# Chunk stage of a hybrid retention and RWKV-7 layer: low-rank products from rounded high parts with the rests stacked over the rows, and outputs and solves of two slabs issued alternately

## The reference, cut to what matters

```python
u = lp['rwkv_w0'][:, None, None, :] + jnp.einsum('btr,drc->dbtc', jnp.tanh(wd), lp['rwkv_w2'])
w = jnp.exp(-jnp.exp(-jax.nn.softplus(-u.astype(jnp.float32)) - 0.5))
a = jax.nn.sigmoid(lp['rwkv_a0'][:, None, None, :] + jnp.einsum('btr,drc->dbtc', ad, lp['rwkv_a2']))
...
def step(s, xt):
    wt, kt, vt, kkt, at = xt[:5]
    sa = jnp.einsum('bhvk,bhk->bhv', s, -kkt)
    s = (s * wt[:, :, None, :] + sa[..., None] * (kkt * at)[:, :, None, :]
         + vt[..., None] * kt[:, :, None, :])
    return s, jnp.einsum('bhvk,bhk->bhv', s, xt[5])
```

## Time and profile before

| what | value |
|---|---|
| median of 3 runs | 4121.16 us (4111.47 to 4129.18) |
| profiled execution, its own time | 4116.76 us |
| span of the profiled execution | 4114.9 us |
| granted TensorE clock, mean | 0.962 |
| busy: PE / DVE / ACT / POOL | 3772.4 / 2290.6 / 1947.2 / 613.5 us |
| chunk stage in the trace | about 1181 to 2225 us |

### The profile page before, as it was taken

The page is one execution under the profiler, slowest core; times in us unless marked ns, Lnnn a source line. Parts: engine busy times, 40 slices in busy tenths (PEclk is TensorE's granted clock), DMA queues, the critical chain, the costliest instruction groups (busy, mean ns, idle before and its releaser), DMA issues. The chain is left out here.

```text
span 4114.9 us, 93756 instructions
## 1 busy us (share of the span) xinstructions
PE 3772.4 (92%) x39634; PEld 3168.5 (77%) x39634; DVE 2290.6 (56%) x3788; ACT 1947.2 (47%) x3029; POOL 613.5 (15%) x601
## 2 busy tenths in 40 slices
PE   7999999999979899989898978997599999999993
PEld 6778878888868788888887767786488888888883
DVE  5533524434337777777776975455554545454445
ACT  5533434434336666666665443243144444444443
POOL 1000000000012122212210333200011111111111
PEclk9999999999989999999998989998699999999997
DMA  7566565555542222222323466654366666666667
GB/s 277 189 180 190 179 194 152 159 155 157 151 119 76 80 76 66 80 80 62 105 64 90 117 222 215 197 181 160 148 210 215 211 213 213 212 217 209 219 209 296
DMA packets 334966, 673.42 MB, mean 164 GB/s; under 512 B 32828, under 2 KB 213156, under 8 KB 316936
## 3 DMA queue, kind: packets, MB, share of 16 engines
q1 hardware_dynamic: 307592, 580.68, 43.3%
q0 software_dynamic: 27008, 87.46, 7.4%
HBM read 524.89 MB, written 143.15 MB: 162 GB/s over the span
## 5 line engine op out<-in xcount | busy, mean ns | idle before, releaser
L112 PE MATMUL fro__acc<-fro__hT_hi,fro__wh 128*128 128x512 f32 (+1 forms) x1608 | 626.0, 389 | 11.8 <-DVE fro__hT_lo L2671 8.9
L113 PE MATMUL fro__acc<-fro__hT_hi,fro__wl 128*128 128x512 f32 (+1 forms) x1608 | 614.3, 382 | 0.0
L114 PE MATMUL fro__acc<-fro__hT_lo,fro__wh 128*128 128x512 f32 (+1 forms) x1608 | 614.1, 382 | 0.0
L2677 DVE TENSOR_TENSOR fro__wl<-prj__w,fro__wh 128x1024 fp32r<-128x1024 f32 x201 | 246.2, 1225 | 640.6 <-ACT fro__wh L2460 640.6
L2088 DVE TENSOR_TENSOR fin__wl<-fin__raw,fin__wh 128x4096 fp32r<-128x4096 f32 x96 | 424.6, 4423 | 318.4 <-ACT fin__wh L2032 318.4
L2032 ACT ACTIVATE fin__wh<-fin__raw 128x4096 fp32r<-128x4096 f32 x96 | 348.4, 3629 | 190.4 <-PE exp__acc L114 190.3
L112 PE MATMUL exp__acc<-fin__wh,exp__xh 128*128 128x512 f32 x1024 | 400.9, 391 | 0.7 <-DVE exp__xl L2093 0.7
L113 PE MATMUL exp__acc<-fin__wh,exp__xl 128*128 128x512 f32 x1024 | 399.3, 390 | 0.0
L114 PE MATMUL exp__acc<-fin__wl,exp__xh 128*128 128x512 f32 x1024 | 399.2, 390 | 0.0
L112 PEld LDWEIGHTS fro__acc<-fro__hT_hi,fro__wh 128*128 128x128 f32 x1608 | 304.7, 189 | 77.9 <-issue 22.2
L113 PEld LDWEIGHTS fro__acc<-fro__hT_hi,fro__wl 128*128 128x128 f32 x1608 | 304.8, 190 | 59.2 <-issue 3.6
(11 more groups left out here) (460 smaller groups left out, 8121.9 us busy)
## 6 DMA issues: line engine op xcount, KB each, us to landing
fin__raw<-in_w_x SPq DMA_DIRECT2D x96, 2048.0 KB
prj__w<-in_w_z SPq DMA_DIRECT2D x201, 512.0 KB, 4.2
s_zT<-fro__pool SPq DMA_DIRECT2D x128, 256.0 KB, 4.7
fro__wm<-in_w_mod POOLq DMA_DIRECT2D x16, 1024.0 KB, 5.6
mix__gate<-s_zT SPq DMA_DIRECT2D x64, 256.0 KB, 4.3
prj__xin<-in_tokens SPq DMA_DIRECT2D x18, 512.0 KB, 5.4
rwc__kS<-s_kS SPq DMA_DIRECT2D x36, 256.0 KB, 3.1
rwc__kkn<-s_kkn SPq DMA_DIRECT2D x36, 256.0 KB, 3.3
```

Source lines behind the costliest of these rows:

```text
L112: pe.matmul(out, sh, mh, start=first, stop=False)
L113: pe.matmul(out, sl, mh, start=False, stop=False)
L114: return pe.matmul(out, sh, ml, start=False, stop=last)
L2677: ve.tensor_tensor(wl[s % 3][:, :, :], w[s % 3][:, :, :], wh[s % 3][:, :, :], ALU.subtract).then_inc(split_lo, 1)
```

## The change

- The operands of the low-rank products become fp32r. Rounded high parts and the rests are stacked over the 128 rows: `lowA` is the rounded weights twice over the rows (from `low_raw`), `zA` the rounded data above and its rest below; `lowB` holds the rest of the weights above, and the bias (rounded in row 64, its rest in row 96) below; `zB` holds the data above and the ones below. Each product of the four becomes two fp32r matmuls that add up in `PB[1]`.
- The parts of the weights are made once (`lowA` on ScalarE, `lowB` on VectorE, `low_parts`), before the first slab. They come by 8 DMAs a direction instead of 4.
- For every slab GpSimd casts `zS` into `zA` (`rounded_rows`), and VectorE makes `zB` and the rest in `zA` with two instructions of 128x256 (`rounded_rows`), after `centred`. The slab's data is loaded by `load_low`, two DMAs as before, one slab earlier.
- `D2`, `e_bk`, `e_rho`, `e_al`, `av`, `kd`, `bb` and `bon` move into `hold["tab"]`, and the loads for the next stage are issued at `h == LAST`.
- `outputs(h-2, 1)` no longer stands between `double(2, h)` and `couple(3, h)`. Where both exist, `outputs_and_solve` issues the eight products of `outputs(h-2, 1)` and the eight of `solve(h-1, 0)` by turns, at the place of `solve`.

```diff
@@ sync @@
+            def load_low(j):
+                for s in range(2):
+                    sp.dma_start(zS[j % 2][side(s), :, :], T["waS"][:, ds(slab_at(j), C)].rearrange("(k p) t -> p k t", k=2)).then_inc(lws[j % 2], 16)
...
             low_rank(1)
             low_rank_rows(1)
+            load_low(1)
             load(1)
+            sp.wait_ge(S["rlo"], at("rlo", 0))
+            load_low(2)
...
-                if h == SLABS - 6:
+                if h == LAST:
+                    for n in ("betad", "kappad", "al", "rho", "bonm"):
+                        sp.wait_ge(S[n], at(n, LAST))
@@ scalar @@
+            for d in range(2):
+                act.wait_ge(low_in[d], 128 + START)
+                act.activation(lowA[:, d, :, :], low_raw[d][:, :, :], ACT.Copy).then_inc(low_hi, 1)
             decays(0)
@@ vector @@
+            def low_parts(d):
+                ve.wait_ge(low_hi, d + 1 + START)
+                ve.tensor_tensor(lowB[0:64, d, :, :], low_raw[d][0:64, :, :], lowA[0:64, d, :, :], ALU.subtract).then_inc(low_lo, 1)
+                ve.wait_ge(low_in[d], 128 + START)
+                ve.tensor_copy(lowB[64:128, d, :, :], low_bias[64:128, d, :, :]).then_inc(low_lo, 1)
+                ve.wait_ge(low_lo, 3 * d + 2 + START)
+                ve.tensor_tensor(lowB[96:128, d, :, :], low_bias[96:128, d, :, :], lowB[96:128, d, :, :], ALU.subtract).then_inc(low_lo, 1)
+            def rounded_rows(j):
+                d = j % 2
+                ve.wait_ge(S["rnd"], at("rnd", j))
+                ve.tensor_scalar(zB[d][:, :, :], zS[d][:, :, :], rows[:, 1:2], rows[:, 2:3], ALU.mult, ALU.add).then_inc(S["rlo"], 1)
+                ve.scalar_tensor_tensor(zA[d][:, :, :], zA[d][:, :, :], rows[:, 0:1], zS[d][:, :, :], ALU.mult, ALU.add).then_inc(S["rlo"], 1)
+            rounded_rows(0)
+            low_parts(0)
+            rounded_rows(1)
+            low_parts(1)
             ve.wait_ge(scan_in, 16 + START)
             running(0)
...
                 if prepare:
                     centred(n)
+                if h + 2 < SLABS:
+                    rounded_rows(h + 2)
@@ tensor @@
                 for q in range(4):
-                    m = mm(f4(PB[1])[:, q, :], w2[:, d, q * P:q * P + P], wS[d][:, :], start=True, stop=True)
+                    c = slice(q * P, q * P + P)
+                    mm(f4(PB[1])[:, q, :], lowA[:, d, 0, c], zA[d][:, 0, :], start=True, stop=False)
+                    m = mm(f4(PB[1])[:, q, :], lowB[:, d, 0, c], zB[d][:, 0, :], start=False, stop=True)
...
+            def outputs_and_solve(j, i):
+                v, z, o = j % B, side(turn_of(j, 1)), side(1 - turn_of(j, 1))
+                x = side(turn_of(i, 0))
+                pe.wait_ge(S["uc1"], at("uc1", j))
+                pe.wait_ge(S["rhc0"], at("rhc0", i))
+                pe.wait_ge(S["gd"], at("gd", i))
+                for n in range(WH):
+                    c = slice(WD * n, WD * n + WD)
+                    y = mm(PB[1][o, c], BK[v][z, n, 1, :], U[1][z, c], start=False, stop=True, skip_group_check=True)
+                    m = mm(PB[0][x, c], Gr[i % 2][x, n // GH, n % GH, :], R[0][x, c], start=True, stop=True)
+                y.then_inc(S["ym1"], 1)
+                m.then_inc(S["uum0"], 1)
...
-                if exists(h - 2):
+                if exists(h - 2) and not exists(p):
                     outputs(h - 2, 1)
                 if inverting:
                     couple(3, h)
-                if exists(p):
+                if exists(h - 2) and exists(p):
+                    outputs_and_solve(h - 2, p)
+                elif exists(p):
                     solve(p, 0)
```

More of the change, by code:

```diff
@@ L161, in rwkv_chunks @@
         scanm = sb("scanm", [P, 4, C])
-        w2 = sb("w2", [P, 2, HALF])
-        a2 = sb("a2", [P, 2, HALF])
+        lowA, lowB = [sb(n, [P, 2, 2, HALF], F32R) for n in ("lowA", "lowB")]
         names = ("kS", "kkn", "kka", "vS", "rS", "rrk")
         ld = [{n: sb(f"{n}{d}", [P, 4, C]) for n in names} for d in range(2)]
-        wS = [sb(f"wS{d}", [P, C]) for d in range(2)]
-        aS = [sb(f"aS{d}", [P, C]) for d in range(2)]
-        sg, L, D, D2, e_bk, e_rho, e_al, av, kd, bb, bon = [sb(n, [P, 4, C]) for n in (
-            "sg", "L", "D", "D2", "e_bk", "e_rho", "e_al", "av", "kd", "bb", "bon")]
+        rows = sb("rows", [P, 3])
+        zS = [sb(f"zS{d}", [P, 2, C]) for d in range(2)]
+        zA, zB = [[sb(f"{n}{d}", [P, 2, C], F32R) for d in range(2)] for n in ("zA", "zB")]
+        sg, L, D = [sb(n, [P, 4, C]) for n in ("sg", "L", "D")]
+        D2, e_bk, e_rho, e_al, av, kd, bb, bon = [
+            hold["tab"][:, n // 2, n % 2 * HALF:n % 2 * HALF + HALF].rearrange("p (q t) -> p q t", q=4) for n in range(8)]
         AR = [sb(f"AR{u}", [P, 4, 2, C]) for u in range(B)]
@@ L186, in rwkv_chunks @@
         bo = sb("bo", [P, C])
+        low_raw = [AR[B - 2 + d][:, :, :, :].rearrange("p q k c -> p (q k c)").rearrange("p (k c) -> p k c", k=2) for d in range(2)]
+        low_bias = BK[B - 1][:, :, :, :].rearrange("p h k c -> p (h k c)").rearrange("p (d k c) -> p d k c", d=2, k=2)
         XB, TP = [[room.ps(f"{n}{g}", [P, 512]) for g in range(NG)] for n in ("XB", "TP")]
@@ L196, in rwkv_chunks @@
         exists = lambda j: 0 <= j < SLABS
-        const_in, scan_in, low_ok, zero_ok, copy_ok = [sem(n) for n in ("const_in", "scan_in", "low_ok", "zero_ok", "copy_ok")]
+        const_in, scan_in, low_ok, zero_ok, copy_ok, low_hi, low_lo = [sem(n) for n in (
+            "const_in", "scan_in", "low_ok", "zero_ok", "copy_ok", "low_hi", "low_lo")]
         lds, lws, low_in = [[sem(f"{n}{d}") for d in range(2)] for n in ("lds", "lws", "low_in")]
@@ L266, in _ @@
                     load(h + 2)
+                if h + 3 < SLABS:
+                    sp.wait_ge(S["rlo"], at("rlo", h + 1))
+                    load_low(h + 3)
                 if h < SLABS:
@@ L293, in _ @@
             for d in range(2):
-                for t in (w2[64:128, d, :], a2[64:128, d, :], wS[d][64:128, :], aS[d][64:128, :]):
-                    gp.memset(t, 0.0)
-                gp.drain()
-                for t in (wS, aS):
-                    gp.memset(t[d][64:65, :], 1.0)
+                gp.memset(low_bias[64:128, d, :, :], 0.0)
                 gp.drain()
                 gp.sem_inc(low_ok, 1)
+            gp.memset(rows[:, :], 0.0)
+            gp.drain()
+            gp.memset(rows[64:128, 0:1], -1.0)
+            gp.drain()
+            gp.memset(rows[0:64, 1:2], 1.0)
+            gp.drain()
+            for r in (64, 96):
+                gp.memset(rows[r:r + 1, 2:3], 1.0)
+                gp.drain()
             for d in range(2):
@@ L337, in _ @@
             rho(0)
+            rounded_rows(2)
             gp.wait_ge(const_in, 16 * NCONST + START)
@@ L346, in _ @@
                 rounded_inverse(h)
+                if h + 3 < SLABS:
+                    rounded_rows(h + 3)
         @block.scalar
@@ L692, in decays @@
                 d = j % 2
[L693 removed]
+                pe.wait_ge(S["rlo"], at("rlo", j))
                 if j:
@@ L705, in learning @@
                 for q in range(4):
-                    m = mm(f4(PB[1])[:, q, :], a2[:, d, q * P:q * P + P], aS[d][:, :], start=True, stop=True)
+                    c = slice(q * P, q * P + P)
+                    mm(f4(PB[1])[:, q, :], lowA[:, d, 1, c], zA[d][:, 1, :], start=True, stop=False)
+                    m = mm(f4(PB[1])[:, q, :], lowB[:, d, 1, c], zB[d][:, 1, :], start=False, stop=True)
                 m.then_inc(S["am"], 1)
```

30 lines of the change are left out of this document (18 added, 12 removed).

## The result

The changed kernel takes 4181.62 us (median of 4 runs, 4177.59 to 4186.2), the kernel before 4116.32 (4 runs, 4106.87 to 4129.18). The ratio is 1.0155, 95% interval 1.0133 to 1.0177: slower by about 65 us. I had forecast 4154 and a range up to 4176. The direction was right; the loss is twice what I had worked out. The time comes near the 4186 of my third rival, but not in its way: the products do overlap, as shown next.

What follows compares the result with a forecast made beforehand. A chain through three engines, none always busy, with ScalarE's `yo`, `U`, `Tb` setting when what follows starts. 0 + 5 + 14.5 + 17 - 3 = +33.5 us on 4121 gave 4154, range 4124 to 4176.

Steps and rivals of the forecast that it cites:

- my third rival: Alternating products of outputs and solve do not overlap, so the group lasts 0.9 us longer: 4186 us; chance 0.08.
- The alternating issue: Outputs and solve in one group: `yo` ends later, delaying `Tb` by 0.415 us mean in 35 iterations, +14.5 us.
- Nothing is gained: At `couple(3)`: the 0.9 us TensorE saves falls where it waits for `Tb` anyway, so the group ends as `solve` did.
- Low-rank products: On TensorE: eight fp32r records take 0.11 us each, as the float32 ones do, so no change, 0 us.
- the 0.24: Low-rank group on TensorE: saving in us a group by the skill's 81 ns a product, an estimate.
- the 0.4: Low-rank group on TensorE: saving in us a group at the low end of 0.06 us a record.
- the rival of 0.06 a record: Low-rank products: the fp32r load is quicker, saving 0.4 us a group, for 4127 us; chance 0.13.
- VectorE, +5: After `centred`: two new 128x256 instructions outlast the idle time by 0.15 us a slab over 34 slabs, +5 us.
- my lower bound: Low end of the VectorE term for the two new instructions after `centred`: 0 us.
- The start, +17: Before the first slab: both directions' weights must be ready first, `key1(0)` comes 17.1 us later; bounds +10 and +20.
- The tables, -3: Next stage's loads moved to the last slab: half of the 6.7 us a slab was longer, -3 us; bounds -7 and 0.
- The low-rank rows' loads: SyncE's `load_low` issued a slab early: counted as nothing.

Runs made afterwards that it cites:

- the late copy: Changed kernel with ScalarE's copy of `yo` moved behind `solved(h-1, 0)` and `copies(4, h)`: 4139.42 us, ratio 1.0056 to the kernel before.
- after_apart: Changed kernel with the products of `outputs(h-2, 1)` back ahead of `couple(3, h)` and `solve(h-1, 0)` alone: 4126.84 us, ratio 1.0035 to the kernel before.
- before_tables_last: Kernel before with the loads for the next stage issued at `h == LAST` instead of `SLABS - 6`: 4110.56 against 4113.23 us, ratio 0.9999.
- start_low_late: apart_start with the DMAs of the low-rank rows back at their old time, one slab later: 4122.14 us, ratio 1.0033 to the kernel before.
- apart_start: after_apart with the second direction's weights prepared later, off the first slab's path: 4114.27 us, ratio 0.9997 to the kernel before.
- before_low_early: Kernel before with only the DMAs of the low-rank rows issued one slab earlier, behind the slab's other loads: 4104.55 against 4113.55 us, ratio 0.9977.

## Why the prediction was wrong

**The alternating issue: I had +14.5, and the runs say 50 to 55.** That is the step that failed. The mechanism that I named is there and has nearly its size: `yo` waits for the group's end, `Tb` comes late, and a slab at full clock grows by 0.32 us where I had 0.415 (27.34 against 27.02, and back to 27.02 with the late copy; the error of the difference is about 0.1). Over 35 slabs that is +11. But the step "TensorE issues 0.9 us less ... Nothing is gained" stopped too early: the sum had no term for the clock. The work taken out and the later `Tb` left more and longer idle times on TensorE at this place, and idle time costs twice: once itself, and once more when the clock falls.

The comparison that isolates this edit is the changed kernel against `after_apart`: the 32 slabs are 921.4 - 878.5 = 42.9 us longer. By the fits of the two traces, 32 x (27.34 - 27.00) = 11 of it is the longer slab, 85.3 x 0.37 - 20.5 x 0.40 = 23 the half clock, and 15.4 x 0.97 - 6.4 x 1.00 = 9 the issue idle, for which no run has a cause. Over all executions the half-clock time is about 100 us longer with the alternating issue (443 against 339, 400 against 304); at the 0.4 us of the fits this makes some 40 us, an estimate, and with 11 for the late copy it comes to the low end of what was measured.

Against the kernel before, the same sum gives the 28 of the 32 slabs: 10 for the slab, 23 for the half clock, and 15.4 x 0.97 - 25.0 x 0.81 = -5 for the issue idle. Of the other two rows, the 7.1 us of the first slabs come with 25 us more of half clock, and the 9.1 us of the tail with the tables' loads, whose move alone made the tail 11.0 longer in `before_tables_last`. The sign was there to see ahead: the earlier trace rows held a slab of 33.8 us, 10 us of it at half clock.

**Low-rank products: right.** A group of eight takes 1.04 us instead of 1.09, the median over the slabs, so it saves 0.05 us and neither the 0.24 nor the 0.4 that the prediction weighs; the rival of 0.06 a record falls. That the load of the weights sets this pace no run tests.

**VectorE, +5: not seen, and not excluded.** The fitted slab without the alternating issue is 27.00 against 27.02, with an error of about 0.1, which is 3 us in 32 slabs. That is my lower bound. My own rows gave 0.23 and 0.44 us, and I took 0.15. The two instructions last 0.41 and 0.48 us, and `levels(1)` starts on average 0.1 us later behind `centred` than before; what made up for it no run takes apart (each low-rank group is 0.05 us shorter).

**The start, +17: right.** +15.6 measured to `centred(0)`, and moving the second direction away gave 12.3 of it back, and 0.38% (16 us) of the time.

**The tables, -3: not seen.** Their slab becomes short and the tail long; I had counted half of that and it is all of it.

**What does not add up.** `after_apart` is 14 us slower than the kernel before, and its terms are 16 for the start, 3 less for the products and about 10 less for the loads (next paragraph), 3 in all. `start_low_late` is 14 slower with only 3.6 us of the start left. All executions of these kernels and of `apart_start` have 17 to 35 us more of half clock than the kernel before (medians of whole programs); at 0.4 us this is 7 to 14, an estimate. What brings it without the alternating issue stays open.

**The low-rank rows' loads: I wrote "nothing" of them.** They move one slab earlier, and that is worth 0.23% by itself in the kernel before (0.09 to 0.37) and 0.36% (1.0033 - 0.9997) between the two kernels with rounded products, which were measured on different chips. It hid part of the loss. PE's idle times put down to issue became fewer, 28 to 15 in `before_low_early`, and more, 15 to 28, in `start_low_late`. In the trace of before, the twelve such idle times of 0.9 us and more end 2.2 to 2.8 us after a packet of the instruction queue began (half of these packets come 3.9 us or more apart), so I take it that TensorE waits there for its program. Why the order of the other loads changes how often, no run shows. The Trainium skill, DMA: Bandwidth & Descriptors, section Queues, rings and completion order, says that a DMA engine serves its queues by turns, packet by packet; by that, loads under way would hold up the program's packets, and no run here measures it.

What stays open besides: which of the idle times, their sum or their length, decides whether the clock falls. The runs moved both at once; the length of a single one does not decide it, as `v_t` shows.
